# Gate and up projections in fp32: nine of eleven weight sets by two nested levels of seven products

## The reference

```python
h = rmsnorm(x, ffn_norm[l])
gu = h @ w_gate_up[l]                       # 1024 x 5632
gt, up = jnp.split(gu, 2, axis=-1)          # D_FF = 2816 each
x = x + (jax.nn.silu(gt) * up) @ w_down[l]  # 2816 x 1024
```

## Time and profile before

| | us |
|---|---|
| median of 3 runs | 3599.18 |
| lowest, highest | 3597.5, 3600.53 |
| span of the profiled execution | 3596.5 |
| TensorE busy in it | 3482.3 |
| VectorE busy | 1885.0 |
| GpSimd busy | 921.6 |

### The profile page before, as it was taken

The page is one execution under the profiler, slowest core; times in us unless marked ns, Lnnn a source line. Parts: engine busy times, 40 slices in busy tenths (PEclk is TensorE's granted clock), DMA queues, the critical chain, the costliest instruction groups (busy, mean ns, idle before and its releaser), DMA issues.

```text
span 3596.5 us, 53959 instructions
## 1 busy us (share of the span) xinstructions
PE 3482.3 (97%) x22362; PEld 2339.3 (65%) x22362; DVE 1885.0 (52%) x3530; ACT 1160.2 (32%) x2185; POOL 921.6 (26%) x736
## 2 busy tenths in 40 slices
PE   7999999999999999999999999999999999999998
PEld 4555555655667977777777756444555545878887
DVE  3555553355445354666666653454777733554543
ACT  3443443222232022333333321775545521110100
POOL 2212221222210003555555510222545430000000
PEclk9999999999999999999999999999999999999999
DMA  5112111101012121111111111221101011221221
GB/s 228 65 74 77 51 65 53 36 36 47 25 46 106 51 85 59 41 44 48 48 48 48 54 71 59 84 76 62 48 31 48 16 74 59 106 89 76 87 81 56
DMA packets 29555, 229.78 MB, mean 64 GB/s; under 512 B 3072, under 2 KB 6784, under 8 KB 9728
## 3 DMA queue, kind: packets, MB, share of 16 engines
q1 hardware_dynamic: 29312, 226.33, 17.0%
HBM read 224.22 MB, written 2.10 MB: 63 GB/s over the span
## 4 chain that ended last, share of the span: by engine, by line
PE 88%; DVE 6%; ACT 3%; issue 2%; DMA 1%; POOL 1%; SPq 0%; DVEq 0%; ACTq 0%; POOLq 0%
PE bank L1295 12%; PE bank L1608 11%; PE bank L1514 7%; PE bank L1950 7%; PE bank L1602 4%; PE bank L1977 4%; PE bank L1729 3%; PE bank L1688 2%; PE bank L1868 2%; PE bank L1420 2%; PE bank L1695 2%; PE bank L1453 2%; PE bank L1242 2%; PE bank L1914 2%; PE bank L1658 1%
## 5 line engine op out<-in xcount | busy, mean ns | idle before, releaser
L1295 PE MATMUL bank<-xT,ring 128*128 128x384 f32 x896 | 323.4, 494 | 2.6 <-ACT Y L2092 2.4
L3615 POOL TENSOR_TENSOR ring<-ring 128x512 f32<-128x512 f32 x112 | 146.8, 1327 | 413.1 <-DMA ring<-in_w 411.3
L3653 POOL TENSOR_TENSOR ring<-ring 128x512 f32<-128x512 f32 x128 | 171.5, 1346 | 285.0 <-DMA ring<-in_w 284.2
L1295 PE MATMUL bank<-hT,ring 128*128 128x384 f32 x672 | 242.8, 493 | 0.0
L1608 PE MATMUL bank<-Y,ring 128*128 128x384 f32 (+1 forms) x768 | 240.7, 457 | 0.0
L1295 PEld LDWEIGHTS bank<-xT,ring 128*128 128x128 f32 x896 | 161.2, 190 | 108.3 <-issue 15.7
L3679 POOL TENSOR_TENSOR arena<-arena 128x512 f32<-128x512 f32 x112 | 184.1, 1643 | 170.8 <-PE bank L1658 155.5
L1608 PE MATMUL bank<-hT,ring 128*128 128x384 f32 (+1 forms) x576 | 184.8, 457 | 9.3 <-DVE arena L3053 8.5
L1729 PE MATMUL bank<-hT,ring 128*128 128x512 f32 x384 | 178.9, 599 | 4.7 <-ACT Y L2067 4.7
L1608 PEld LDWEIGHTS bank<-Y,ring 128*128 128x128 f32 x768 | 141.2, 190 | 64.8
L1295 PEld LDWEIGHTS bank<-hT,ring 128*128 128x128 f32 x672 | 121.4, 190 | 80.9 <-issue 16.0
(11 more groups left out here) (588 smaller groups left out, 7506.4 us busy)
## 6 DMA issues: line engine op xcount, KB each, us to landing
ring<-in_w SPq DMA_DIRECT2D x77, 1024.0 KB, 4.8
ring<-in_w SPq DMA_DIRECT2D x35, 2048.0 KB, 8.5
ring<-in_w SPq DMA_DIRECT2D x20, 1280.0 KB, 5.5
ring<-in_w SPq DMA_DIRECT2D x10, 1536.0 KB, 7.9
ring<-in_w SPq DMA_DIRECT2D x8, 1408.0 KB, 5.9
ring<-in_w SPq DMA_DIRECT2D x6, 512.0 KB, 3.5
xT<-in_xT SPq DMA_DIRECT2D x1, 3072.0 KB, 14.9
xT<-in_xT SPq DMA_DIRECT2D x4, 512.0 KB, 7.2
```

The costliest lines, as they stand in the source:

```text
L1295: ins = e.matmul(bank[spot["st", kind, n, at]][:, 0:384], left[:, k], right[:, k], start=first and k == 0, stop=k == 3, skip_group_check=True)
L3615: e.tensor_tensor(s[:, i], l, r, op).then_inc(up("st_s", (kind, n, i)), 1)
L3653: e.tensor_tensor(s[:, i], l, r, op).then_inc(up("gs_s", (kind, n, i)), 1)
```

## The change

Sets 0 and 1 stay as they are. For sets 2 to 10 each of the seven outer products (now of 512 by 256 weights and 512 by 256 activations for a whole set) is itself made by seven inner products of 256 by 128 and 256 by 128: `gq`, 98 matmuls of 128 columns a set. An inner product's results z are not put together at once: bank pairs gather them (four z of 128 columns in one bank, three in the next), products that share an outer term run on in the same banks, and two bank pairs are **seeded**: ScalarE copies product 0's banks into those of product 2, and product 2's into those of product 4, and the next product accumulates on top (`gq_c`). In the first set four identity matmuls in two pairs write these banks beforehand. VectorE adds two pairs of banks to what ScalarE has copied out (`gq_v`) and puts all together in seven operations (`gq_u`, 128 x 2 x 2 x 128), after which Silu and the product with up are one operation each for a set (`gq_z`, `gq_p`).

Inner weight sums, four of 256 columns a product, are VectorE's for outer products 0, 3, 5 and GpSimd's for 1, 2, 4, 6 (`gq_i`), in four cells each: the sums of a product wait for the product four before it. Outer weight sums are four of 1024 columns (`gq_s`). The inner sums of activations are made once (`gq_t`), into parts of xT and Y; six of x's blocks go out to DRAM for that and come back (`x_out`, `x_again`). The activation differences for down are made in large pieces in the last set (`down_t`), down's first four weight sums are GpSimd's, and the products of down(0) go in the order 0, 4, 2, 1, 3, 5, 6.

```diff
 def gate_up_steps():
 
-    made = [("gu", 0), ("gu_t",), ("gu_s", 1)]
-    for j in range(1, 22):
-        made += [("gu_s", j + 1)] * (j < 21) + [("gu", j)]
-    return made + [("down_s", 0, 0), ("down_s", 0, 1), ("gu_p", 21), ("down_s", 0, 2), ("down_s", 0, 3)]
+    made = [("gu", 0), ("x_out",), ("gu_t",), ("gu_s", 1), ("gu_s", 2), ("gu", 1), ("gu_s", 3), ("gq_i", 2, 0), ("gq_t", 0), ("gu", 2)]
+    made += [("gq_t", 1), ("gq_s", 2, 0), ("gq_i", 2, 1), ("gq_s", 2, 1), ("gq_i", 2, 2), ("gu", 3), ("gu_p", 3)]
+    for s in range(2, 11):
+        first, last = s == 2, s == 10
+        made += [("gq", s, 0)] + [("gq_c", s - 1, 4)] * (not first) + [("gq_c", s, 0), ("gq_s", s, 2), ("gq_s", s, 3), ("gq_i", s, 3)]
+        made += [("gq_u", s - 1)] * (not first) + [("gq_i", s, 4), ("gq", s, 1)] + [("gq_z", s - 1)] * (not first)
+        made += [("gq_c", s, 1), ("gq_i", s, 5)] + [("gq_s", s + 1, 0)] * (not last) + [("gq_p", s - 1)] * (not first)
+        made += [("gq", s, 2), ("gq_c", s, 2), ("gq_i", s, 6)] + [("gq_s", s + 1, 1)] * (not last) + [("down_t", 0)] * last
+        made += [("gq", s, 3), ("gq_c", s, 3)] + [("gq_i", s + 1, 0)] * (not last)
+        made += [("gq", s, 4), ("gq_v", s, 0)] + [("gq_i", s + 1, 1)] * (not last) + [("down_t", 1)] * last
+        made += [("gq", s, 5), ("gq_v", s, 1)] + [("gq_i", s + 1, 2)] * (not last) + [("down_t", 2), ("down_s", 0, 2)] * last
+        made += [("gq", s, 6)]
+    return made + [("x_again",), ("gq_c", 10, 4), ("gq_u", 10), ("gq_z", 10), ("down_s", 0, 0), ("down_s", 0, 1),
+                   ("gq_p", 10), ("down_t", 3), ("down_s", 0, 3)]
 
...
+            def gq(s, i):
...
+                top = {0: 0, 1: 4, 2: 2, 3: 0, 4: 6, 5: 4, 6: 6}[i]
+                if i in (0, 1, 2, 4):
+                    for b in (top, top + 1):
+                        take(b, ("gq", s, i, b), {0: ("gq_c", (s, 3)), 1: ("gq_v", (s, 1)), 2: ("gq_c", (s, 2)), 4: ("gq_c", (s, 4))}[i])
+                if s == GQ_FIRST and i in (2, 4):
+                    for b, n in ((top, 256), (top + 1, 128)):
+                        ins = e.matmul(bank[b][:, 256:256 + n], ident, hT[:, 0, 0:n], start=False, stop=True, skip_group_check=True)
+                    ins.then_inc(up("gq_bits", i), 1)
+                if i == 2:
+                    q.wait_ge(*on("gq_c", (s, 0)))
+                if i == 3:
+                    q.wait_ge(*on("gq_c", (s, 0)))
+                if i == 4:
+                    q.wait_ge(*on("gq_d", s))
+                if i == 5:
+                    q.wait_ge(*on("gq_c", (s, 1)))
+                if i == 6:
+                    q.wait_ge(*on("gq_v", (s, 0)))
+                if i in (1, 2, 4, 5):
+                    q.wait_ge(*on("gq_s", (s, {1: 0, 2: 1, 4: 2, 5: 3}[i])))
+                (x11, x12, _, x22), (s1, s2, s3, s4) = gq_blocks(gq_left(s, i)), gq_cell(s, i)
+                right, (t1, t2, t3, t4) = gq_right(i)
+                y11, _, y21, y22 = right[:, 0:2, 0:128], None, right[:, 2:4, 0:128], right[:, 2:4, 128:256]
+                for z, l, r in ((0, x11, y11), (4, x12, y21), (5, x22, t4), (1, s2, t2), (2, s3, t3), (3, s1, t1), (6, s4, y22)):
+                    if z == 5:
+                        q.wait_ge(*on("gq_t", ("b", 7) if i in (0, 3, 5) else ("t", 3)))
+                    if z == 1:
+                        q.wait_ge(*on(*gq_inner(s, i)))
...
+                    for k in range(2):
+                        ins = e.matmul(o, l[:, k], r[:, k], start=i in (0, 1) and z in (0, 4) and k == 0, stop=k == 1,
+                                       skip_group_check=True)
+                ins.then_inc(up("gq_mm", (s, i)), 1)
+                if i == 6:
+                    give("gu", "gq_mm", (s, 6))
...
                 a, b, c, d = (take(4 * (p % 2) + n, ("down", p, n), ("down_u", (p, i)))[:, 0:256] for n, i in enumerate((3, 0, 5, 4)))
-                for n, (m, l, r, first) in enumerate((
-                        (a, g_lo, [yf[:, k, h1] for k in range(11)], True), (b, s2, t2, True), (d, s3, t3, True), (c, s1, t1, True),
+                ways = ((a, g_lo, [yf[:, k, h1] for k in range(11)], True), (b, s2, t2, True), (d, s3, t3, True), (c, s1, t1, True),
                         (a, g_hi, [yf[:, k, h1] for k in range(11, 22)], False), (d, u_hi, t4, False),
-                        (c, s4, [yf[:, k, h2] for k in range(11, 22)], False))):
+                        (c, s4, [yf[:, k, h2] for k in range(11, 22)], False))
+                for n in range(7) if p else (0, 4, 2, 1, 3, 5, 6):
+                    m, l, r, first = ways[n]
                     if n in (1, 2, 3, 6):
...
+                        q.wait_ge(*on(*down_sum(p, {1: 1, 2: 2, 3: 0, 6: 3}[n])))
                     elif n:
                         q.wait_ge(*(on("down_p1", p) if n == 4 else on("down_u", (p, 1))))
                     if n == 6:
...
+            def gq_c(s, n):
+
+                q.wait_ge(*on("gq_mm", (s, {0: 0, 1: 1, 2: 2, 3: 3, 4: 6}[n])))
+                if s == GQ_FIRST and n in (0, 2):
+                    for i in (3, 4):
+                        q.wait_ge(*on("gu_u", (2 if n == 0 else 3, i)))
+                    q.wait_ge(*on("gq_bits", 2 + n))
+                if s > GQ_FIRST and n == 1:
+                    q.wait_ge(*on("gq_u", (s - 1, 6)))
...
+                src = {0: 0, 1: 4, 2: 2, 3: 0, 4: 6}[n]
+                lo, hi = bank[src], bank[src + 1][:, 0:384]
+                if n in (0, 2):
+                    to = 2 if n == 0 else 6
+                    e.activation(bank[to], lo, ACT.Copy)
+                    e.activation(bank[to + 1][:, 0:384], hi, ACT.Copy).then_inc(up("gq_c" if n == 0 else "gq_d", (s, 0) if n == 0 else s), 1)
+                if n:
+                    v = gq_V[:, 896 * {1: 3, 2: 1, 3: 0, 4: 2}[n]:][:, 0:896]
+                    e.activation(v[:, 0:512], lo, ACT.Copy)
+                    e.activation(v[:, 512:896], hi, ACT.Copy).then_inc(up("gq_c", (s, n)), 1)
...
+            def gq_silu(s):
+                q.wait_ge(*on("gq_u", (s, 6)))
+                e.activation(yf[:, 2 * s:2 * s + 2, :], gq_GU[:, 0:1024].rearrange("p (r t) -> p r t", r=2),
+                             ACT.Silu).then_inc(up("gq_z", s), 1)
...
+            def gq_t(n):
+
+                q.wait_ge(*on("x_kept"))
...
+                    x11, x12, x21, x22 = (gu_T[:, :, 2 * k:2 * k + 2, 128 * t:128 * t + 128] for k in range(2) for t in range(2))
+                    for i, l, r, w in ((0, x12, x11, None), (1, x22, gq_TT[0], 0), (2, x22, x12, None), (3, x21, gq_TT[1], 1)):
+                        q.wait_ge(*on("gu_t", 3))
+                        if w is not None:
+                            q.wait_ge(*on("gq_t", ("t", w)))
+                        e.tensor_tensor(gq_TT[i], l, r, ALU.subtract).then_inc(up("gq_t", ("t", i)), 1)
...
+            def gq_s(s, n):
...
+                q.wait_ge(*(on("gq_mm", (s - 1, (1, 2, 4, 5)[n])) if s > GQ_FIRST else on("gu_mm", (2 if n < 2 else 3, 6))))
+                if n in (1, 3):
+                    q.wait_ge(*on("gq_s", (s, n // 2)))
+                l, r, op = ((u_lo, u_hi, ALU.add), (gq_S[:, 0], g_lo, ALU.subtract), (g_lo, u_lo, ALU.subtract),
+                            (g_hi, gq_S[:, 1], ALU.subtract))[n]
+                e.tensor_tensor(gq_S[:, n], l, r, op).then_inc(up("gq_s", (s, n)), 1)
...
+            def gq_i(s, i):
+                if i not in GQ_DVE:
...
+                (x11, x12, x21, x22), c = gq_blocks(gq_left(s, i)), gq_cell(s, i)
+                a = spot["gu_slab", s]
+                q.wait_ge(*on(f"w{slot_of(a)}", a))
...
+                for n, (o, l, r, op) in enumerate(((0, x21, x22, ALU.add), (2, x11, x21, ALU.subtract), (1, c[0], x11, ALU.subtract),
+                                                   (3, x12, c[1], ALU.subtract))):
...
+                    e.tensor_tensor(c[o], l, r, op).then_inc(up("gq_iv", (s, i, n)), 1)
+
+            def gq_v(s, n):
+
+                o, top = (3, 6) if n == 0 else (1, 4)
+                q.wait_ge(*on("gq_mm", (s, 4 + n)))
+                q.wait_ge(*on("gq_c", (s, 1 + n)))
+                v = gq_V[:, 896 * o:896 * o + 896]
+                e.tensor_tensor(v[:, 0:512], bank[top], v[:, 0:512], ALU.add).then_inc(up("gq_v", (s, n, 0)), 1)
...
+                e.tensor_tensor(v[:, 512:896], bank[top + 1][:, 0:384], v[:, 512:896], ALU.add).then_inc(up("gq_v", (s, n)), 1)
...
+            def gq_u(s):
...
+                for n, (o, l, r, w) in enumerate(((c12, gq_all(0), gq_all(1), None), (c11, gq_all(0), gq_all(4), None),
+                                                  (c21, c12, gq_all(2), 0), (c12, c12, gq_all(3), 0), (c22, c21, gq_all(3), 2),
+                                                  (c12, c12, gq_all(6), 3), (c21, c21, gq_all(5), 4))):
+                    if w is not None:
+                        q.wait_ge(*on("gq_u", (s, w)))
+                    e.tensor_tensor(o, l, r, ALU.add).then_inc(up("gq_u", (s, n)), 1)
...
+            def gq_p(s):
...
```

(33 more changed lines are left out.)

## The result

| us | before | changed |
|---|---|---|
| median of 7 runs | 3600.29 | 3610.73 |
| lowest, highest | 3597.5, 3601.11 | 3607.16, 3611.91 |
| span of the profiled execution | 3596.5 | 3605.4 |

The ratio is 1.0031, with a 95% interval of 1.0021 to 1.0041: slower by 0.31%, about 10 us. The profiled execution of the changed kernel was the fastest of its seven, 3607.16.

A forecast was written before the change was run, and what follows sets the result against it. TensorE's streamed columns bound the kernel until VectorE, held by GpSimd, needs more a set. Terms -20.3 + 1.3 + 2.8 + 11.2 + 1.8 + 10.2 = +7.0 give span 3603.5, time 3606; range 3589 to 3622.

The forecast's parts named there:

- The four places where TensorE waits: Before a set's seventh product, at the first set's ScalarE bank copies, at half-set 2, before down's second product.
- TensorE's work (-20.3): Gate and up: 196 instructions of 128 columns take 21.9 us a set, 2.26 less, over nine sets: -20.3 us.
- The rival of the weight load: Weight loads of 190 ns pace 128-column instructions: 37.2 us a set, +138, time 3744; within the remaining 0.03.
- The first set (+4.1): First changed set: four identity matmuls 1.3 us, plus two waits for ScalarE's copies between banks, 2.8 us.
- VectorE with GpSimd (23.5 a set, +11.2): VectorE's 17.0 us plus 6.5 of lock collisions with GpSimd exceed TensorE's 21.9; seven sets at 1.6 give +11.2.
- thirteen collisions at 0.50: In a set, 13 of GpSimd's 16 sums each hold a VectorE operation for 0.50 us: 6.5 us.
- Head (+1.8): Half-set 2: VectorE does set 2's sums before combining, so TensorE's sixth product there waits: +1.8 us.
- Tail (+10.2): Passage into down: VectorE's queue, then Silu, table load and copy delay down's second product: TensorE waits 10.2 us.
- E: End of the last gate and up product, from which the prediction counts the tail's times.
- The sum: Adds work, first set, collisions, head and tail: +7.0 us, span 3603.5, time 3606.

The follow-up runs named there:

- e1b_no_read: Changed kernel with GpSimd's sixteen inner weight sums a set replaced by fills with zero, so GpSimd writes but reads nothing; 3596.19 us, ratio 0.9991.
- e3b_tail: Changed kernel with the passage into down reordered, down's first four sums on VectorE, table load behind down's first copy; 3603.93 us, ratio 1.0014.

## Why the prediction was right, point by point

- **Direction, size, range.** 3606 was forecast, as most likely slower; 3610.7 was measured, in the range, slower by 0.31%. The four places where TensorE waits and what it waits for there were right. The size owes something to luck: a term that the sum lacked (7.1 us) was in part made up for by waits that were forecast too long (4.4).
- **TensorE's work (-20.3).** Right: 201.0 us for nine sets with VectorE out of the way, of which 3.9 are the first set's extras; 197.1 is nine times 21.9. The rival of the weight load had no part: 196 instructions with their loads take 22.16 us after a wait. The rule of the Trainium skill that stood beside it ("TensorE: Matmul & The Clock Gate", "The mechanism") says that a load overlaps running matmuls only on another row group; that row contradicts it as L1514 did. The same section of the Trainium skill also names a background weight buffer; no run here tells whether that is what lets the loads overlap.
- **The first set (+4.1).** 3.9: each pair of matmuls and its wait is 1.94 us.
- **VectorE with GpSimd (23.5 a set, +11.2).** The mechanism was right and the size of VectorE's work nearly so, a little high: 22.6 to 23.3 a set. Own work was 16.4 (17.0 in the sum) and what GpSimd adds is 6.2 to 6.9 (6.5 in the sum, thirteen collisions at 0.50); how many collisions that is wasn't counted. The set lasts 23.95 in the mean all the same, because VectorE stands idle 0.9 to 1.25 us in it for a TensorE that has lost clock. The trace agrees with the rule of the Trainium skill that stood beside it ("SBUF — State Buffer", "SBUF: two separate sides"): 1.2 against 0.68 at L3709, and 0.68 again where GpSimd reads nothing.
- **What was left out: the clock.** The forecast let TensorE wait 1.6 us in each of seven sets at full clock. It waits 2.1 in four, and three of these are followed by 1.6 us of slow instructions. The extra over e1b_no_read is 15.0: 8.3 of waits, 4.9 of clock, the rest refilling and short stops. Sum 11.2, measured 15.0.
- **Head (+1.8).** 1.5.
- **Tail (+10.2).** The wait was 8.7, as VectorE's last combines ended at E + 10.8 (12.0 forecast); the slow product behind it adds 2.2, so 11.3 in all. TensorE went on at E + 13.7, which had been put at E + 15.0. That VectorE's queue and not ScalarE's makes most of the wait is borne out by e3b_tail: 5.2 us against 1.3.
- **The sum.** +7.0 was forecast for the stages and +11.4 measured. The missing 4.4: in the sets 4.9 of clock and 1.8 of refilling and short stops, less 2.9 of waits that were fewer and less 0.2 in the first set; in the tail 2.2 of clock and 0.4 of small stops, less 1.5 of wait; less 0.3 in the head. The weak step is thus the clock, 7.1 us that no term of the sum stood for: TensorE was taken to go on at full speed behind every wait. In the span 2.5 us are hidden by the early arrival ahead of the change, in the medians they are not.

## What to carry over

Idle time of an engine is not free if its work makes another engine's longer: count the moved work at what it adds to the other engine (here 0.39 to 0.52 us a sum) against what it saves there (0.37). When TensorE's work shrinks until it meets another engine's queue, look for the stretch behind each new wait as well as for the wait: here 7.1 us beside 20.5 of waits stood in instructions that count as busy. And where a product ends a stage, put in the other queues first what the next product needs; large pieces that are wanted later go behind it.

## What the runs showed of the hardware

- Idle time of TensorE can cost more than itself. 0.9 us cost nothing beyond it and some 0.27 of refilling; of nine waits of 1.95 us, 26 to 28 us apart, every second one was followed by 1.69 us of loss; of nine of 3.6 us seven, by 1.69 or 2.7. In the rows after such a wait eight 128-column instructions take 1.61, 1.73 or 1.83 in place of 1.16, and the granted clock of 3323.9 to 3327.9 is 0.57 in the mean, that is mostly its level of 1.2 GHz, where it is 1.00 after the wait at 3277.50:

```profile
3323.90:3327.90 4.00, 4.00 (x21) 4.00 (x22) 3.79 (x4) 0.00 (x0) 2.63 (x3) 0.57 0.01 4
...
3277.50:3281.50 4.00, 4.00 (x35) 4.00 (x36) 4.00 (x5) 0.57 (x2) 2.66 (x3) 1.00 0.01 4
```

- GpSimd's sum of 256 columns (L4018) takes 0.72 us at least and one of 1408 columns (L4030) 3.2 to 4.0; a fill of 256 takes 0.31, and beside 144 of them no combine and no inner sum of VectorE was longer.
- VectorE's reads of a bank are not held: with GpSimd at work in the same sets, L3693 (512 columns) takes 0.69 us at most and L3694 (384) 0.55.
- ScalarE copies from bank to bank as fast as from bank to SBUF: 0.58 us for 512 columns and 0.47 for 384, against 0.60 and 0.48. The forecast had kept open that it might take half as long again.
- Matmuls of 128 columns in f32 keep a pace of 111.8 ns an instruction, weight loads included, over whole sets (178.50 us for 1596, e1b_no_read).
